# Dot products read the normalised inputs from PSUM; a sixth place for first-table rows

## The reference

```python
def peer(x, w_q, sub_keys, expert_u, expert_v):
    ...
    top_s, top_i = lax.top_k(s, PEER_TOPK)
    ...
    best_s, pos = lax.top_k(cand_s, PEER_TOPK)
    ids = jnp.take_along_axis(cand_i, pos, axis=-1)
    g = jax.nn.softmax(best_s, axis=-1).astype(x.dtype)
    def block(args):
        xt, it, gt = args
        u = jnp.take(expert_u, it, axis=0)
        act = jax.nn.gelu(jnp.einsum('td,tkd->tk', xt, u)) * gt
        v = jnp.take(expert_v, it, axis=0)
        return jnp.einsum('tk,tkd->td', act, v)
```

## Time and profile before

| | us |
|---|---|
| median of 3 runs (3437.86 to 3445.06) | 3438.97 |
| the profiled execution | 3439.91 |
| its span | 3438.1 |
| DVE busy in the span | 2586.6 |
| PE busy in the span | 2977.6 |
| POOL busy in the span | 850.1 |
| dots (L3042): 256, mean 2.289 each, busy | 584.4 |
| gathers of U (L3178): 256, mean 1.699 each, busy | 434.9 |

### The profile page before, as it was taken

How to read it: one execution, slowest core, us unless ns; L and a number is a source line. 1 busy time by engine, 2 the same in 40 slices (tenths; PEclk the granted TensorE clock), 3 DMA queues, 4 the chain that set the end, 5 groups by cost and what they waited for, 6 DMA issues and landing times.

```text
span 3438.1 us, 37676 instructions
## 1 busy us (share of the span) xinstructions
PE 2977.6 (87%) x14064; PEld 2399.8 (70%) x14064; DVE 2586.6 (75%) x3898; ACT 1690.7 (49%) x2757; POOL 850.1 (25%) x549
## 2 busy tenths in 40 slices
PE   8999999999999999999999999975533434489998
PEld 7998988888888888888888888722212311466776
DVE  7786777775557877885557676899888887678997
ACT  6554555554445555554446752223444663644444
POOL 0000000000000000000000002687868886245653
PEclk9999999999999999999999999997865557589999
DMA  6554555546555555555566478999999999679997
GB/s 233 169 148 154 156 182 173 170 164 204 185 183 185 184 194 184 184 188 204 193 204 198 159 245 297 376 385 403 402 366 400 407 399 416 231 282 354 382 388 280
DMA packets 426647, 877.50 MB, mean 255 GB/s; under 512 B 18811, under 2 KB 249116, under 8 KB 392928
## 3 DMA queue, kind: packets, MB, share of 16 engines
q1 hardware_dynamic: 347208, 453.16, 39.5%
q0 software_dynamic: 78240, 421.56, 31.3%
q10 hardware_dynamic: 1016, 0.35, 0.0%
HBM read 872.91 MB, written 2.10 MB: 255 GB/s over the span
## 4 chain that ended last, share of the span: by engine, by line
PE 70%; POOL 10%; DMA 9%; DVE 6%; issue 4%; ACT 2%; DVEq 0%; SPq 0%; ACTq 0%; POOLq 0%
PE W L1753 14%; PE W L1761 11%; PE W L1763 11%; PE W L1762 11%; PE W L1751 7%; POOL Ub L3178 7%; PE W L1933 5%; DMA Ub<-in_peer_u,ids 4%; DMA Vr<-in_peer_v 3%; DVE Ub L3042 2%; PE M L1900 2%; DMA Vx<-in_peer_v,vid 2%; POOL Vx L3193 2%; PE T L1929 1%; PE M L1814 1%
## 5 line engine op out<-in xcount | busy, mean ns | idle before, releaser
L2604 DVE TENSOR_TENSOR wl<-raw,wh 128x1024 fp32r<-128x1024 f32 (+1 forms) x720 | 850.4, 1186 | 563.4 <-ACT wh L2065 561.7
L2065 ACT ACTIVATE wh<-raw 128x1024 fp32r<-128x1024 f32 (+1 forms) x720 | 740.6, 1031 | 893.8 <-PE W L1763 573.5
L1753 PE MATMUL W<-u,wh 128*128 128x512 f32 x2040 | 722.5, 397 | 0.0
L3042 DVE CUSTOM_DVE_ANT_0 Ub<-Ub,xn 128x2048 f32<-128x2048 f32 x256 | 584.4, 2289 | 122.7 <-DMA Ub<-in_peer_u,ids 118.1
L1751 PE MATMUL W<-u,wl 128*128 128x256 f32 x2176 | 603.0, 282 | 0.2 <-DVE u L2566 0.2
L3178 POOL DMA_INDIRECT Ub<-in_peer_u,ids x256 | 434.9, 1699 | 297.8 <-DVE dots L3042 146.1
L1753 PEld LDWEIGHTS W<-u,wh 128*128 128x128 f32 x2040 | 383.3, 188 | 88.3
L1761 PE MATMUL W<-wh,u 128*128 128x512 f32 (+1 forms) x1152 | 436.2, 379 | 1.2 <-DVE u L2964 1.0
L1763 PE MATMUL W<-wh,u 128*128 128x512 f32 (+1 forms) x1152 | 427.9, 371 | 0.0
L1762 PE MATMUL W<-wl,u 128*128 128x512 f32 (+1 forms) x1152 | 427.6, 371 | 0.0
L1751 PEld LDWEIGHTS W<-u,wl 128*128 128x128 f32 x2176 | 410.7, 189 | 6.4 <-issue 0.5
(11 more groups left out here) (400 smaller groups left out, 5067.2 us busy)
## 6 DMA issues: line engine op xcount, KB each, us to landing
raw<-in_w_in SPq DMA_DIRECT2D x128, 1024.0 KB, 5.1
raw<-in_w_up SPq DMA_DIRECT2D x88, 1024.0 KB, 4.8
Vr<-in_peer_v SPq DMA_DIRECT2D x128, 512.0 KB
raw<-in_w_down SPq DMA_DIRECT2D x44, 1024.0 KB, 5.0
raw<-in_w_in SPq DMA_DIRECT2D x144, 256.0 KB, 3.4
raw<-in_w_out SPq DMA_DIRECT2D x32, 1024.0 KB, 5.0
raw<-in_w_proj_a SPq DMA_DIRECT2D x16, 1024.0 KB, 4.9
Wb<-in_peer_w_q SPq DMA_DIRECT2D x16, 1024.0 KB, 6.7
```

The source lines that it names most:

```text
L1753: i = q.matmul(o, vh, u[:, :, kk, :], start=False, stop=last)
L2065: q.activation(wh[:, s % NS, 0:b.half], r, ACT.Copy).then_inc(s_hi, 1)
L2604: q.tensor_tensor(wl[:, s % NS, 0:b.half], r, wh[:, s % NS, 0:b.half].bitcast(F32), SUB).then_inc(s_lo, 1)
L3042: q.tensor_tensor_reduce(U[:, :], U[:, :], xn[:, t, :], 1.0, 0.0, MUL, ADD, dots[t][:, k:k + 1]).then_inc(s_dot, 1)
```

## The change

Half 0's normalised input is copied once from SBUF into the four banks W0 to W3 by ACT (`copy_xn`), and from the first dot that the planner's clocks put behind the copy (`self.wide`, here dot 29) the dots read their second input from there. Half 1's input is made by DVE directly in these banks, in front of dot 128 and after dot 127. The 8 KB per partition that it had in SBUF are the place `Ub5` (NU = 6, a new `U_SETS`). The turns of ids and activations move from W0 and W1 to T0 and T1, and with them the waits of `turn_ids`, `turn_act`, `build`, `one_hot` and `spike`; the first dense product waits for dot 255.

```diff
-NU = 5
+NU = 6
-U_SETS = ((48, (0, 1, 2, 3)), (206, (0, 1, 2, 3, 4)), (236, (0, 2, 3, 4)), (256, (2, 3, 4)))
+U_SETS = ((48, (0, 1, 2, 3)), (206, (0, 1, 2, 3, 4, 5)), (236, (0, 2, 3, 4, 5)), (256, (2, 3, 4, 5)))
...
     def dot(self, n, landed):
         self.in_order("dot", n)
+        if self.wide is None and n >= 128 or self.copied is not None and max(self.clock["DVE"], landed) > self.copied:
+            self.wide = n if self.wide is None else self.wide
         self.dotted[n] = self.put("DVE", 2.55, landed, "dot", n)
...
-            if dot is not None:
+            if dot is not None and (n != 128 or self.when(("xn", 1, 3)) is not None):
                 options.append((dot, "dot"))
...
-            if self.when("streamed") is not None and self.when(("xn", 1, 3)) is None and n >= 8:
-                options.append((c["DVE"] - 0.2, "xn"))
+            if n == 128 and self.when(("xn", 1, 3)) is None:
+                dot = None
+                options.append((c["DVE"], "xn"))
+            if self.copied is None:
+                options.append((c["ACT"], "copy"))
...
-        xn = area.get("xn", [2, D])
+        xn = area.get("xn", [D])
+        area.o += 4 * D
...
-        Ub += [area.get("Ub1", [D]), at("Ub2", [D], u0), at("Ub3", [D], u0 + 16384), at("Ub4", [D], u0 + 8192)]
+        Ub += [area.get("Ub1", [D]), at("Ub2", [D], u0), at("Ub3", [D], u0 + 16384), at("Ub4", [D], u0 + 8192), at("Ub5", [D], Z + 8192)]
...
+        wide_x = ctx.enter_context(nc.psum_tensor("W", [P, D], F32))
+        banks = {f"W{i}": wide_x[:, 512 * i:512 * i + 512] for i in range(4)}
...
             def mul(j):
                 if j == 0:
-                    e.wait_ge(s_turnk, 4)
+                    e.wait_ge(s_dot, 256)
...
+            def copy_xn():
+                e.wait_ge(s_xn, 4)
+                for b in (-2, -1):
+                    e.wait_ge(s_pair[(len(blocks) + b) % 2], plan.pair[b] + 2)
+                for j in range(4):
+                    i = q.activation(banks[f"W{j}"][:, :], xn[:, CK[j]], ACT.Copy)
+                i.then_inc(s_turnk, 1)
...
             def xn_part(t, j):
                 e.wait_ge(s_g2, 16)
                 e.wait_ge(s_rstd, 12)
                 if t:
-                    e.wait_ge(s_taken, chunk_used(4))
-                q.scalar_tensor_tensor(xn[:, t, CK[j]], X[:, t, CK[j]], rstd[:, t:t + 1], g2[:, CK[j]],
+                    e.wait_ge(s_turnk, 1)
+                    e.wait_ge(s_dot, 128)
+                q.scalar_tensor_tensor((wide_x if t else xn)[:, CK[j]], X[:, t, CK[j]], rstd[:, t:t + 1], g2[:, CK[j]],
                                        MUL, MUL).then_inc(s_xn, 1)
...
             def dot(n):
                 t, k = divmod(n, 128)
-                place, used, _ = u_place(n)
-                U = Ub[place]
+                U = Ub[u_place(n)[0]]
                 e.wait_ge(s_xn, 4 * (t + 1))
-                e.wait_ge(s_u[place], 16 * (used + 1))
-                q.tensor_tensor_reduce(U[:, :], U[:, :], xn[:, t, :], 1.0, 0.0, MUL, ADD, dots[t][:, k:k + 1]).then_inc(s_dot, 1)
+                e.wait_ge(*u_landed(n))
+                if n >= plan.wide:
+                    e.wait_ge(s_turnk, 1)
+                inputs = wide_x if n >= plan.wide else xn
+                q.tensor_tensor_reduce(U[:, :], U[:, :], inputs[:, :], 1.0, 0.0, MUL, ADD, dots[t][:, k:k + 1]).then_inc(s_dot, 1)
```

More of the change, by code:

```diff
@@ L1080, in products @@
                 self.weigh(g)
+            elif what == "copy":
+                self.copied = self.put("ACT", 2.2, 0.0, "copy_xn")
             elif what == "xn":
@@ L1163, in lay @@
         self.asked = self.chosen = self.got_v = 0
+        self.wide = self.copied = None
         self.u_in, self.v_in, self.dotted, self.acted, self.spreads = {}, {}, {}, {}, {}
@@ L1407, in program @@
         Vb += [at(f"Vy{i}", [HALF], Z + 16384 + 4096 * i) for i in range(NB)]
-        banks = {n: ctx.enter_context(nc.psum_tensor(n, [P, 512], F32))
-                 for n in ("W0", "W1", "W2", "W3", "T0", "T1", "M0", "M1")}
+        wide_x = ctx.enter_context(nc.psum_tensor("W", [P, D], F32))
+        banks = {f"W{i}": wide_x[:, 512 * i:512 * i + 512] for i in range(4)}
+        banks.update({n: ctx.enter_context(nc.psum_tensor(n, [P, 512], F32)) for n in ("T0", "T1", "M0", "M1")})
         T0, T1, M0, M1 = (banks[n] for n in ("T0", "T1", "M0", "M1"))
@@ L1444, in program @@
         s_first = sem("first_head")
-        s_u, s_place = [sem(f"u{i}") for i in range(NU)], [sem(f"row{i}") for i in range(NE)]
+        s_u, s_place = [sem(f"u{i}") for i in range(NU - 1)] + [s_cos], [sem(f"row{i}") for i in range(NE)]
         s_dot, s_dgelu, s_dact, s_diag, s_spread, s_out = (
@@ L1497, in keeps, with u_landed @@
             return s_bank[bank.name], bank.n + i // 2
+        def u_landed(n):
+            place, used, _ = u_place(n)
+            return s_u[place], 16 * (used + 1) + 16 * (place == NU - 1)
         def landed(kind, i):
@@ L1904, in turn_ids @@
                 e.wait_ge(s_ids, 8 * t + 8)
[L1905 to L1911, removed]
-            def turn_act(t):
[L1914 to L1920, removed]
+                e.wait_ge(*keeps(32 * t))
+                q.transpose(T0[:, 0:P], idf[t][:, 0, :], ident[:, :])
+                q.transpose(T0[:, P:2 * P], idf[t][:, 1, :], ident[:, :]).then_inc(s_turn, 1)
+            def turn_act(t):
+                e.wait_ge(*keeps(32 * t + 1))
+                e.wait_ge(s_dact, 32 + BUILT // GROUP if t else 32)
+                k = BUILT if t else P
+                q.transpose(T1[0:k, 0:P], dots[t][:, 0:k], ident[:, :]).then_inc(s_turn, 1)
             def build(i):
@@ L1925, in build @@
                 e.wait_ge(s_hot, i + 1)
+                e.wait_ge(s_turnk, 2 * t + 3)
                 e.wait_ge(s_spa if on_act(i) else s_spd, spike_count(i))
@@ L2355, in turn_ids @@
                 e.wait_ge(s_turn, 2 * t + 1)
-                q.activation(idT[t][:, :, :], banks["W0"][:, 0:2 * P].rearrange("p (j k) -> p j k", j=2), ACT.Copy).then_inc(s_turnk, 1)
+                q.activation(idT[t][:, :, :], T0[:, 0:2 * P].rearrange("p (j k) -> p j k", j=2), ACT.Copy).then_inc(s_turnk, 1)
             def turn_act(t):
@@ L2361, in turn_act @@
                 e.wait_ge(s_turn, 2 * t + 2)
-                q.activation(actT[t][0:k, :], banks["W1"][0:k, 0:P], ACT.Copy).then_inc(s_turnk, 1)
+                q.activation(actT[t][0:k, :], T1[0:k, 0:P], ACT.Copy).then_inc(s_turnk, 1)
             def peaks(out, k, t, j, g):
@@ L2375, in one_hot @@
                 e.wait_ge(s_iota, 32 + 16 * t)
-                e.wait_ge(s_turnk, 2 * t + 1)
+                e.wait_ge(s_turnk, 2 * t + 2)
                 if t:
@@ L2475, in scalar @@
                   "keep_scores": keep_scores,
-                  "top_exp": top_exp, "gelu": gelu, "spread": spread, "turn_ids": turn_ids, "turn_act": turn_act,
+                  "copy_xn": copy_xn, "top_exp": top_exp, "gelu": gelu, "spread": spread, "turn_ids": turn_ids, "turn_act": turn_act,
                   "one_hot": one_hot, "spike": spike, "keep": keep_group, "high": high, "upper": upper, "close": close})
@@ L3170, in get_u @@
                 e.wait_ge(s_ids, n // 16 + 1)
-                place, used, last = u_place(n)
+                place, _, last = u_place(n)
                 if n < 2 or n in U_CHUNKS:
```

## The result

Median after 3400.31 us (3396.19 to 3405.22, 4 runs), before 3438.41 us (3428.78 to 3445.06, 4 runs): ratio 0.9892, 95% interval 0.9864 to 0.992. The change gains 38 us; the forecast was 17.5, and the range ended 5 us above the time. The profiled executions are 41.7 us apart (3439.9 and 3398.2).

The account below looks back on a forecast made before the run. It took the loop of dot done, place free, POOL issue, landing and dot as bounding up to dot 239. Stretch gains 2.7 + 8.4 + 4.2 + 4.2 - 2.0 = 17.5 us gave 3422 us, range 3405 to 3439.

Parts of the forecast that it names:

- rival C: A dot reading four PSUM banks takes longer than 2.29 us; at 0.3 us more, 3454 us; chance 0.06.
- 62 cycles more for a PSUM source: Estimated 65 ns a dot, 14 us of DVE time in 211 dots; half on the path makes the sum 7 us worse.
- 2240 to 2360: DVE limits; moving half 1's xn chunks out of this stretch gains 2.7 us, bounds 0 and 8.5.
- 2360 to 2600: Transfers rise from 382 to 396 GB/s for 91.7 MB: gain 8.4 us, bounds 0 and 25.
- xn at dot 128: Half 1's xn, 2.73 us on DVE, now stands between dots 127 and 128: loss 2 us, bounds 0 and 3.
- 2600 to 2820: Transfers rise from 410 to 418 GB/s for 90.2 MB: gain 4.2 us, bounds 0 and 8.
- 2820 to 2940: Transfers rise from 397 to 411 GB/s for 47.6 MB: gain 4.2 us, bounds 0 and 8.
- half way: For 2360 to 2600, 396 GB/s was taken, half way from 382 to the next stretch's 410.
- Rival D: The queue is never short and all four stretches run at 420 GB/s or more: 3407 us, chance 0.13.
- DVE is the limit: In 2240 to 2360, choosing experts and dots keep DVE busy 111.55 of 120 us; gain only 2.7 us.
- Rival A: Transfers were full anyway, so a longer queue adds nothing; xn's move and the last stretch count: 3438 us, chance 0.15.
- B: POOL stays held because dots still write products to SBUF; only the sixth place acts: 3433 us, chance 0.10.

Follow-up runs that it names:

- e3_sbuf5: The changed kernel with all dots reading SBUF, five places and the old U_SETS, so only the order and the turns remain: 3443.88 us, ratio 1.0009.
- e2_sbuf6: The changed kernel with all dots reading SBUF and the sixth place in other memory, for steps 48 to 189: 3431.11 us, ratio 0.9969.
- e1_psum5: The changed kernel without its sixth place (old U_SETS, five places), dots still reading PSUM: 3404.46 us, ratio 0.9892.
- e4_psum6_190: The changed kernel, dots reading PSUM, with the sixth place for steps 48 to 189 alone: 3402.79 us, ratio 0.9883.
- e5_hold_long: Five places, dots reading PSUM, plus a 1150-column POOL memset (1.07 us) that each chosen U and V gather waits for: 3507.07 us, ratio 1.0196.
- e6_hold_short: Five places, dots reading PSUM, plus a 350-column POOL memset (0.40 us) that each chosen gather waits for: 3416.28 us, ratio 0.993.
- e9_hold_matched: Five places, dots reading PSUM, with awaited POOL memsets before gathers, 575 columns up to step 120 and 1280 after: 3447.61 us, ratio 1.0016.

## Why the prediction was right in kind and short by half

Right: faster; POOL's issue as what ended last; the gather at 0.94 us instead of 2.18; POOL near half load (89.4 us for 96 gathers, with 0.3 between them 118 of 220 us; forecast 111 for 89); dot 239 as the place where the gain is read; nothing from the copy, the turns and the groups. Against rival C, a dot from four banks is 5 ns shorter, not longer. The Trainium skill's "VectorE: DVE Perf Modes", section "The TRN2 errata", has 62 cycles more for a PSUM source. No run here shows them (2284 against 2289 ns), so its 7 us don't enter.

The terms, from the starts of the dots in the two profiled executions:

| step | forecast us | measured us |
|---|---|---|
| 2240 to 2360 (to dot 57, which started at 2360 before) | 2.7 | 6.8, with 1.9 that stood at dot 29 already |
| 2360 to 2600 (dots 57 to 127) | 8.4 | 16.4 |
| xn at dot 128 | -2.0 | -2.9 |
| 2600 to 2820 (dots 128 to 206) | 4.2 | 6.1 |
| 2820 to 2940 (dots 206 to 239) | 4.2 | 11.2 |
| sum at dot 239 (rounded) | 17.5 | 37.5 |

**The step that failed is the rates "half way".** I took 396 GB/s for 2360 to 2600, half of the way from 382 to 410, which was itself a rate of the late POOL; and 418 and 411 for the next two, half of the way up to 426. They became 410, 426 and, over dots 206 to 239, 421. The best rate was in front of me: 426 in 2880 to 2900. The prediction had also found that POOL, full with 214 of 220 us, would fall to half. With the late engine at half load and, from 2360 on, only the DMA itself named as late next, the rate to take was the best one seen, not a mean with the rate of the fault. Halving the gap had no row behind it. Rival D, which did this sum at 420, gave 3407 us. With the measured rates in it (414, 410, 426 and 421) the prediction's own sum comes to 5.2 + 16.4 + 8.3 + 6.9 - 2.9 = 34 of the 37.5 us: the mechanism was right, and these terms were too small.

**The second error is "DVE is the limit" in 2240 to 2360.** It was 93% busy there, and I let that stretch gain 2.7 us. It ran at 414 GB/s instead of 396, and DVE was busy 115.66 us instead of 111.55. A high share of busy time was taken for a bound over the stretch, but over dots 32 to 127 DVE was idle 49 us, 39 of them waiting for landings, and it gave 19 of the 49. The 39 us free after 2360 were listed and not used in the sum.

**The third is the last stretch, 4.2 us forecast and 11.2 measured.** Rivals A and B put what they gave it down to the fourth and fifth place. From dot 206 to 239, before took 111.6 us, e3_sbuf5 111.2, e2_sbuf6 111.9; e1_psum5, with the old places there and short gathers, 103.9; the changed kernel 100.4. So most of it, some 7 to 8 us, is the short gather. About half of the 11.2 us goes with some 2.5 MB that were moved less (398 x 112 = 44.6 MB, 421 x 100 = 42.1): POOL's gathers in this stretch are 42 instead of 48 by the windows above. Why is left open.

Not shown: that 4 us more came between the last dot and the end of the profiled span (417.4 us before, 413.5 after). The products of the dense stage took 392.7 us from first to last before and 388.8 after, and in the twelve experiments 399.2 in one (e4_psum6_190) and 389.8 to 395.8 in the others; I take it for scatter. At 38.1 us the medians agree with the 37.8 at dot 255.

Rival A falls, and B with its mechanism: shares of 1.00 hid 410 against 426 GB/s. Rival A's text counts three of four stretches at 1.00, but the earlier trace rows has two, with 0.97 and 0.98 beside them. The remark that speaks against the change, in the Trainium skill's "SBUF — State Buffer", section "Who interferes with whom", that `tensor_tensor` did not stall a DMA, doesn't hold for these gathers beside a product with two SBUF inputs: e3_sbuf5 and e1_psum5 differ in the inputs' place, a median of 1908 against 936 ns a gather goes with it, and 39 us.

## What to carry to other kernels

Look at what stands beside each DMA issue on POOL. If a DVE instruction with two SBUF inputs holds it, putting one input into PSUM freed the issue here (2.1 to 0.94 us) without making the DVE instruction longer; one more buffer, where that can't be done, bought back a third of it (13 of 39 us). Once the late step is at half load, cost the freed stage at the best rate the trace shows anywhere, and ask for a named limiter before taking less; two cures for one wait are not to be added. And when a delay is put in to imitate a wait, look at what it does to the other engines and compare stretch by stretch: a total can match by two errors.

## What was not expected of the hardware

A DMA share of 1.00 or 1.01 stood beside rates from 396 to 426 GB/s (before 396 and 410; e3_sbuf5 409; changed 414 and 426): the share doesn't show a short queue, the GB/s do. Gathers, most of them of U's 8 KB rows, kept 426 GB/s over 220 us with POOL idle for 60% of it. And a memset on POOL isn't free for DVE: `TENSOR_SCALAR pi<-pos` of 128x16 took at most 200 ns in e1_psum5 and up to 1774 beside memsets of 1.07 us in e5_hold_long, while a dot with its input in PSUM stayed at 2284 ns in e1_psum5, e6_hold_short and e9_hold_matched. e6_hold_short lost 12 us although POOL had 93 of 220 us free in 2600 to 2820 and that window ran at 425 GB/s: 8 of them stand in dots 32 to 127, among the choosing steps, and 3 of these 8 are DVE's longer busy time.
